# Mixture-of-experts stage: `down` one expert behind, scatter two behind, a ring of 18 weight blocks

## What is computed

```python
def moe(h, router_w, router_b, w_gate, w_up, w_down):
    ...
    # sigmoid affinities, best group of 4 experts, top 2 of it, weights w (T x 16)
    for e in range(N_EXPERTS):
        he = (jax.nn.silu(x @ w_gate[e]) * (x @ w_up[e])) @ w_down[e]
        y = y + w[:, e:e + 1] * he
```

## Time and profile before

| What | Value |
|---|---|
| Device time, median of 3 runs | 1356.97 us (1355.93 to 1357.9) |
| Profiled execution, span | 1355.8 us; the page gives no time of its own around it |
| TensorE busy | 1284.2 us (95%), 6716 matmuls |
| VectorE busy, ScalarE busy | 733.1 us (54%), 538.7 us (40%) |
| First matmul of gate and up, layers 0 and 1 | 236.10 us, 646.81 us |
| SP's queue of DMAs (q1) | 331.57 MB, 65.0% of 16 engines' span |
| Chain that ended last | TensorE 85%; L1358 15%, L1392 8% of the span |

### The profile page before, as it was taken

How to read it: one execution, slowest core, us unless ns; L and a number is a source line. 1 busy time by engine, 2 the same in 40 slices (tenths; PEclk the granted TensorE clock), 3 DMA queues, 4 the chain that set the end, 5 groups by cost and what they waited for, 6 DMA issues and landing times.

```text
span 1355.8 us, 16753 instructions
## 1 busy us (share of the span) xinstructions
PE 1284.2 (95%) x6716; PEld 891.1 (66%) x6716; DVE 733.1 (54%) x1199; ACT 538.7 (40%) x787; POOL 74.5 (5%) x78
## 2 busy tenths in 40 slices
PE   6999998999999799898999999699999998899998
PEld 5887886344443487676444443378888877899986
DVE  4766657233322585886332222566674566578772
ACT  4445443111111343682211111455556654465551
POOL 0000000000000000000000000005670000000000
PEclk9999998999999799998999999799999999899999
DMA  9653458999999664307999999765455336355540
GB/s 338 207 180 131 156 217 371 391 420 421 422 422 420 245 200 165 139 1 326 386 421 421 422 420 421 286 191 172 134 172 166 125 124 196 131 187 186 187 156 31
DMA packets 103890, 342.51 MB, mean 253 GB/s; under 512 B 10188, under 2 KB 17020, under 8 KB 79100
## 3 DMA queue, kind: packets, MB, share of 16 engines
q1 hardware_dynamic: 97056, 331.57, 65.0%
q10 hardware_dynamic: 6748, 9.77, 2.1%
HBM read 340.27 MB, written 1.05 MB: 252 GB/s over the span
## 4 chain that ended last, share of the span: by engine, by line
PE 85%; DVE 7%; DMA 3%; ACT 3%; issue 1%; ACTq 1%; DVEq 0%
PE PS L689 23%; PE PS L1358 15%; PE PS L536 10%; PE PS L1392 8%; PE PS L614 7%; PE PS L592 5%; PE PS L1340 2%; DMA moe_more<-in_moe_w_up 2%; PE PS L1402 2%; PE PS L1368 1%; PE PS L2041 1%; DVE wlo L501 1%; PE PS L673 1%; PE PS L1768 1%; ACT whi L495 1%
## 5 line engine op out<-in xcount | busy, mean ns | idle before, releaser
L501 DVE TENSOR_TENSOR wlo<-raw,whi 128x2048 fp32r<-128x2048 f32 (+1 forms) x122 | 273.8, 2264 | 113.6 <-ACT whi L495 109.0
L495 ACT ACTIVATE whi<-raw 128x2048 fp32r<-128x2048 f32 (+1 forms) x122 | 224.8, 1875 | 32.8 <-PE PS L592 13.9
L689 PE MATMUL PS<-whi,th 128*128 128x512 f32 x480 | 191.2, 398 | 3.1 <-DVE wlo L501 1.8
L689 PE MATMUL PS<-whi,tl 128*128 128x512 f32 x480 | 187.3, 390 | 0.0
L689 PE MATMUL PS<-wlo,th 128*128 128x512 f32 x480 | 187.0, 389 | 0.0
L1358 PE MATMUL PS<-moe_ring,xg 128*64 128x512 f32 x768 | 170.1, 593 | 0.0
L1358 PEld LDWEIGHTS PS<-moe_ring,xg 128*64 128x64 f32 x768 | 54.8, 137 | 108.0 <-issue 107.8
L1494 DVE SCALAR_TENSOR_TENSOR y_split<-PS,w_slot,y_split 64x512 fp32r<-64x512 f32 x64 | 48.0, 750 | 135.9 <-ACT y_split L1456 134.9
L1523 DVE TENSOR_TENSOR hidden<-hidden,PS 64x512 f32<-64x512 f32 x32 | 22.1, 691 | 165.5 <-ACT hidden L1465 165.5
L689 PEld LDWEIGHTS PS<-whi,th 128*128 128x128 f32 x480 | 90.2, 188 | 23.9 <-DVE wlo L501 2.7
L689 PEld LDWEIGHTS PS<-whi,tl 128*128 128x128 f32 x480 | 90.1, 188 | 19.1
(11 more groups left out here) (408 smaller groups left out, 1986.0 us busy)
## 6 DMA issues: line engine op xcount, KB each, us to landing
moe_ring<-in_moe_w_gate SPq DMA_DIRECT2D x48, 1024.0 KB, 15.2
moe_ring<-in_moe_w_up SPq DMA_DIRECT2D x48, 1024.0 KB, 17.0
moe_ring<-in_moe_w_down SPq DMA_DIRECT2D x48, 1024.0 KB, 15.7
raw<-in_w_in SPq DMA_DIRECT2D x32, 1024.0 KB, 5.3
raw<-in_ret_w_in SPq DMA_DIRECT2D x24, 1024.0 KB, 5.2
raw<-in_w_up SPq DMA_DIRECT2D x20, 1024.0 KB, 5.2
raw<-in_w_down SPq DMA_DIRECT2D x10, 1024.0 KB, 5.0
raw<-in_ret_w_out SPq DMA_DIRECT2D x8, 1024.0 KB, 5.0
```

Source lines behind the costliest of these rows:

```text
L495: nc.scalar.activation(s.whi[:, high, 0:kc, 0:wide], s.raw[:, slot, 0:kc, 0:wide], ACT.Copy).then_inc(s.hi_done, 1)
L501: nc.vector.tensor_tensor(s.wlo[:, slot, 0:kc, 0:wide], s.raw[:, slot, 0:kc, 0:wide], s.whi[:, high, 0:kc, 0:wide], ALU.subtract).then_inc ...
L689: last = nc.tensor.matmul(PS[:, 2 * (col % 2) + tt, 0:wide], x[:, KC * kb + c, tt * P:(tt + 1) * P], w[:, k, c, 0:wide], start=(kb == 0 an ...
```

## The change

The expert loop is staggered: in turn e TensorE now does gate and up of e, slot weights of e + 1, both halves of scatter(e - 2), the gather, `down(e - 1)` and then the turns of e. For the last expert the turns precede `down(14)`, and scatter(14) stands between the halves of `down(15)`, which uses bank 7 and keeps its turned rows in a free part of `xg`. The product is written in two operations of 64 x 256, one to the upper and one to the lower 64 partitions, so `hidden` is 128 x 256 and is turned with two full transposes instead of four. The blocks are numbered in the order of use (`gate_up_at`, `down_at`). The ring gets two `tail` slots at an address that no earlier stage uses, 18 in all; the order of homes puts tail, three raw, one high and the two `more` buffers first, and `more` now waits for the mixer's last output (`ret_o_lo`, `nsa_out_lo`), not for its whole output product. To make room the tensors start at byte 640 of a partition, not 16512, with `dynamic_dma_scratch_size=512`.

```diff
-MOE_SLOTS = 16
+MOE_SLOTS = 18
...
-        moe_homes = [("raw", 0), ("raw", 1), ("raw", 2), ("high", 0), ("raw", 3), ("high", 1), ("raw", 4), ("high", 2),
-                     ("raw", 5), ("high", 3), ("raw", 6), ("high", 4), ("more", 0), ("more", 1),
+        moe_homes = [("tail", 0), ("tail", 1), ("raw", 0), ("raw", 1), ("raw", 2), ("high", 0), ("more", 0), ("more", 1),
+                     ("raw", 3), ("high", 1), ("raw", 4), ("high", 2), ("raw", 5), ("high", 3), ("raw", 6), ("high", 4),
                      ("turned", 0), ("turned", 1)]
...
+        def gate_up_at(e):
+            return 6 * e - 2 if e else 0
+        def down_at(e):
+            return 6 * e + 8 if e + 1 < E else 6 * e + 4
...
-                else:
-                    sp.wait_ge(block_used, b0)
+                elif kind == "more":
+                    if layer == 0:
+                        sp.wait_ge(ret_o_lo, RET_H)
+                    else:
+                        sp.wait_ge(nsa_out_lo, 4)
...
             def turned_hidden(e):
                 pe.wait_ge(s.h_done, v0 + e + 1)
-                rows = hidden[:, :].rearrange("p (b q c) -> p b c q", b=2, c=2)
-                for k in range(4):
+                rows = hidden[:, SEQ:2 * SEQ].rearrange("p (q c) -> p c q", c=2)
+                for c in range(2):
...
                 if e == 0:
                     pe.wait_ge(s.wg_out, table_count(layer))
+                    slot_weights(0, 6)
+                if e + 1 < E:
+                    if e >= 1:
+                        pe.wait_ge(s.hT_done, v0 + e)
+                    slot_weights(e + 1, gate_up_bank(e + 1))
+                if e >= 2:
+                    for tt in range(TT):
+                        scatter(e - 2, tt)
                 if g < E // PER:
                     gather(g, j, 7)
...
+                if e == E - 1:
+                    turned_hidden(e)
...
-                down(e)
+                if e >= 1:
+                    for b in range(2):
+                        down(e - 1, b)
+                if e < E - 1:
+                    turned_hidden(e)
+            down(E - 1, 0)
+            for tt in range(TT):
+                scatter(E - 2, tt)
+            down(E - 1, 1)
             for tt in range(TT):
                 scatter(E - 1, tt)
...
+                if e == E - 1:
+                    turned(e)
+                if e >= 1:
+                    y(e - 1)
+                if e < E - 1:
+                    turned(e)
+            y(E - 1)
...
-                nc.vector.tensor_tensor(hidden[0:SLOTS, :], hidden[SLOTS:2 * SLOTS, :],
-                                        PS[SLOTS:2 * SLOTS, gate_up_bank(e), :], ALU.mult).then_inc(s.h_done, 1)
+                nc.vector.tensor_tensor(hidden[0:SLOTS, SEQ:2 * SEQ], hidden[SLOTS:2 * SLOTS, 0:SEQ],
+                                        PS[SLOTS:2 * SLOTS, gate_up_bank(e), 0:SEQ], ALU.mult)
+                nc.vector.tensor_tensor(hidden[SLOTS:2 * SLOTS, SEQ:2 * SEQ], hidden[SLOTS:2 * SLOTS, SEQ:2 * SEQ],
+                                        PS[SLOTS:2 * SLOTS, gate_up_bank(e), SEQ:2 * SEQ],
+                                        ALU.mult).then_inc(s.h_done, 1)
```

More of the change, by code:

```diff
@@ L1315, in gate_up_bank, with down_bank_of, hT_of @@
             return 4 + e % 2
+        def down_bank_of(e):
+            return 6 if e + 1 < E else 7
+        def hT_of(e):
+            return hT if e + 1 < E else xg[:, 0, 0]
         XG = 2 + PER * (E // PER - 1)
@@ L1346, in gate_and_up @@
             def gate_and_up(e, half):
-                g, u = 6 * e + 2 * half, 6 * e + 2 * half + 1
-                moe_landed(pe, layer, 3 * e + half)
+                g, u = gate_up_at(e) + 2 * half, gate_up_at(e) + 2 * half + 1
+                moe_landed(pe, layer, g // 2)
                 if e < PER:
@@ L1381, in slot_weights, with down @@
                                  start=True, stop=True).then_inc(s.wg_done, 1)
[L1383 to L1390, removed]
-                        for half in range(2):
-                            m = nc.tensor.matmul(PS[64 * half:64 * half + 64, 6, :], hT[:, 2 * b + c, :],
-                                                 moe_place(layer, n)[:, 2 * c + half, :], start=(b == 0 and c == 0),
-                                                 stop=(b == 1 and c == 1), skip_group_check=True)
-                    m.then_inc(moe_used, 1)
+            def down(e, b):
+                if b == 0:
+                    pe.wait_ge(s.hT_done, v0 + e + 1)
+                    if 1 <= e < E - 1:
+                        pe.wait_ge(s.y_lo, 2 * (v0 + e))
+                    moe_landed(pe, layer, down_at(e) // 2)
+                for c in range(2):
+                    for half in range(2):
+                        m = nc.tensor.matmul(PS[64 * half:64 * half + 64, down_bank_of(e), :], hT_of(e)[:, 2 * b + c, :],
+                                             moe_place(layer, down_at(e) + b)[:, 2 * c + half, :],
+                                             start=(b == 0 and c == 0), stop=(b == 1 and c == 1),
+                                             skip_group_check=True)
+                m.then_inc(moe_used, 1)
             def scatter(e, tt):
@@ L1493, in y @@
                     dve.wait_ge(s.y_hi, 2 * (v0 + e) + half + 1)
-                    nc.vector.scalar_tensor_tensor(y_split[low, half, :], PS[rows, 6, :], w_slot[rows, e:e + 1],
+                    nc.vector.scalar_tensor_tensor(y_split[low, half, :], PS[rows, down_bank_of(e), :],
+                                                   w_slot[rows, e:e + 1],
                                                    y_split[rows, half, :], ALU.mult, ALU.subtract).then_inc(s.y_lo, 1)
```

65 lines of the change are left out of this document (33 added, 32 removed).

## The result

The changed kernel took 1360.43 us (median of 19 runs, 1357.7 to 1362.9), the kernel before, run beside it, 1357.58 (19 runs). The ratio is 1.0019 with a 95% interval of 1.0013 to 1.0026: 2.85 us or 0.2% slower, a small loss that the interval sets apart from no change. The forecast was 1353.2 us, its range 1349.0 to 1358.3. The profiled execution of after took 1360.88 us, with a span of 1358.9.

What follows compares the result with a forecast made beforehand. TensorE was taken to set the pace, with DMA just fast enough. Gains of 1.56 us in layer 0 and 2.23 in layer 1, together 3.8, gave 1356.97 - 3.8 = 1353.2 us; 80% range 1349.0 to 1358.3.

Steps and rivals of the forecast that it cites:

- TensorE's order: Expert stages, by start times: layer 0 gains 1.56 us, layer 1 2.23 with its 0.67 us wait, together 3.8 us.
- Rival (3): Expert stages: dearer switches or later y(14) take back 1 to 2 us a layer, 1355 to 1357 us; chance 0.18.
- The weight stream: Expert weight loads: last block lands at about 437, 5 us earlier; DMA stops being a bound, layer 1's wait goes.
- What else moves: Outside TensorE's sum: next stage's raw blocks, new addresses and smaller scratch cost nothing, early loads at most 1 us.
- rival (4): The next stage's raw blocks come 3 us or more too late on each layer, 1357 to 1361 us; chance 0.05.
- Rival (1): Clock falls in expert 0's idle time, 5.1 us a layer: 1363.4 us for both layers, 1358.3 for one; chance 0.12.
- Rival (2): The second round of switches per expert is free: 12.98 us an expert, 1346.5 us in all; chance 0.09.

Runs made afterwards that it cites:

- The fills: Dummy work in the changed kernel: matmuls in expert 0's hole, ratio 1.0002; transposes in idle time at 1112, 1.0006; both, 0.9995. Transposes in the kernel before: 0.9992.

## Why the prediction was wrong

Two steps of it failed, the size of the order's gain and the clock, and both pushed the time up.

**"TensorE's order": the sum was 3.8 us, the traces have 0.9 to 1.55.** Its steps held in kind and came out a little short in sum. Gate and up of expert 1 began at +11.90 us instead of +11.73. An expert with a gather takes 13.34 us, not 13.30: gate and up 7.02 and `down` 3.58 are as forecast, scatter 0.93 (0.94), but slot weights take 0.33 (0.24) and the turns 0.43 (0.40), against a gather of 1.05 (1.12). One without takes 12.39 instead of 12.34. Over thirteen experts that is 0.6 us, and with 0.2 from experts 0 and 1 gate and up of expert 15 begins 0.8 us late (+194.91 for +194.1). Behind it y(14) and the wait of the turns cost 0.3 more than the 17.95 us forecast. Together 1.1 us a layer: the gain of 1.56 and 2.23 became 0.44 and 1.11. Layer 1's 0.67 us of it was a wait of one execution, which before does not always have. Errors of 0.04 us in a term that comes ten times and of 0.2 to 0.3 us at the two ends were as large as most of the gain. Rival (3) named this, at the same size of 1 to 2 us a layer. The sum also set the two turns against the second round of switches, 0.23 us for 0.23, and so never asked what the turns bring without the order. The runs answer it: 211.27 us a stage, where the whole change has 213.17.

**"The weight stream": right in that it stops being a bound, unproven as a gain.** No gate and up or `down` in after waits for DMA, and the two stages differ only by the clock. The ring alone shows both stages at 213.60, but before with new addresses has the same 213.61 twice with its ring of 16. The last block landed at about 441.3, not 437, and is wanted after 445; with the hole filled and no fall there the last packets end at 438.7. That eight early blocks meet nothing is not as sure: undoing four of them gave 1 to 2 us, within the intervals.

**"What else moves": right where it was tested.** Addresses and scratch measured nothing. ScalarE's first two splits take 3.71 us as before and start straight behind the last y (453.01 in layer 0, 863.80 in layer 1), with no wait for a block; rival (4) is out.

**Rival (1), the clock in expert 0's hole, came on top**, at a chance of 0.12 and left out of the sum. The hole was forecast as "about 245.6 to 247.8" and is 2.21 us long. The step that failed is the limit that I read from two rows, with the hole "the shorter of them": 2.95 us of idle time with a fall and 2.50 us without one do not mean that 2.2 us are safe. The row at 1112.7 that stood against a fall was itself a matter of the execution: with two turns, the ring or the addresses alone, which leave this work as it is, 3.4 us at 1.2 GHz stand there. Its price was off the other way. I took ten microseconds at half clock, 5.1 us; the fall in the hole is 3.4 us long and costs 1.7 (5.35 for 3.65 us), and it came in one layer of two in both profiled executions of after. The forecast of 1363.4 for two falls was therefore too dear. That the measured time lies between it and the 1358.3 for one fall is luck: it came out of a smaller gain, a cheaper fall and the one at 1113, which the forecast had only in its 2 us for falls that shift between the stages.

**The forecast's sum, put right:** 1357.6 (before, run beside it) - 0.9 to 1.55 (the stages) + 1.7 (fall in expert 0) + 0 to 1.6 (what the fall at 1113 takes more from after than from before) + 0.4 to 1.1 (the starts of the two layers, by the two executions of after against one of before) = 1358.2 to 1361.1 us, against 1360.4 measured. The fills support the second and third terms, the last one rests on single executions, and the sum is not sharper than that. How much of the 2.85 us belongs to the hole, to 1113 and to the starts stays open. Rival (2), a free second switch, is out: the middle expert is 13.34 us, not 12.98, and the second round costs 0.23.

## What to carry to other kernels

A deeper software pipeline moves its stalls to its first and last step; read those as carefully as the middle. Here the order won 0.7 us in each of three experts a layer and paid as much in the ten before them, and the two ends, with a hole of 2.2 us in the first expert and waits of 1.2 us in the last, made it a loss of 1.9 us. When TensorE is nearly always busy, a new idle time of 2 us costs more than itself, because the clock may fall behind it; look for work that is ready and can be started there (here one gate and up moved ahead of the turns, worth 6.6 us by the medians, of which 4.4 are the stages' own) before counting what an order gains. And measure the parts, against a kernel that has been changed the same way otherwise: of three that were changed together, two turns instead of four carried the gain that the times show.

## What the runs showed of the hardware

- An idle time of 2.2 us on TensorE, with full work on both sides, dropped the granted clock to 1.2 GHz for 3.4 us in layer 0 of all four profiled executions that have it, and in layer 1 of one of the four; in the other three it stayed at 2.4 GHz. The Trainium skill ("TensorE: Matmul & The Clock Gate", The HAM clock gate) names idle time as the cause; the rows agree, and add that the length of one idle time does not decide alone.
- Seven matmuls of no use in that hole, in each layer, made the program 2.3 us faster (1.0002 against 1.0019), although they cost some 1.7 us elsewhere.
- Each round of leaving 64-column matmuls for full-array work and going back cost 0.23 us (13.34 us an expert with two rounds, 13.12 with one, otherwise the same matmuls).
- Work that no edit touches lost its clock in some executions and not in others (3.4, 6.8 us or nothing at 1106 to 1113; 3.4 us and nothing in the two of the filled hole, which are one kernel). One profiled execution of a kernel is one sample; the mean clock that each run gives (median 0.971 in 19 runs of after, 0.973 to 0.974 in before) told more than the two profiles.
- With the DMA engines full (382 GB/s over 452 to 460), TensorE began a ready operation 2.0 to 2.3 us late, with no wait shown, in layer 0 of all three executions with the hole filled. Two packets of the instruction queue lay side by side there and took 1.8 to 2.1 us in place of 1.0 to 1.2. The cause was not tried.
